# Activations streamed by even and then odd 64-byte lines in the 256-column projections

## The reference, cut to what matters

```python
def swiglu(h, w_gu, w_down):
    g, u = jnp.split(h @ w_gu, 2, axis=-1)
    return (jax.nn.silu(g) * u) @ w_down          # w_down: 2816 x 1024
# layers 0 and 1: h += .5*norm(swiglu(norm(h))); h += norm(mixer(norm(h))); h += .5*norm(swiglu(norm(h)))
# layer 2 (256 tokens):
merged = (jax.nn.sigmoid(gate_a) * (o_a @ w_br_dsa)       # 512 x 1024
          + jax.nn.sigmoid(gate_b) * (o_b @ w_br_moba))   # 512 x 1024
x = x + gt_m * (merged @ w_out)                           # 1024 x 1024
x = x + gt_f * ((jax.nn.silu(g_ff) * u_ff) @ w_down)      # 2816 x 1024
```

## Time and profile before

| | us |
|---|---|
| median of 3 runs | 1467.04 |
| the profiled execution | 1465.28 |
| its span, first to last instruction | 1463.4 |
| TensorE busy with MATMULs | 1441.8 (99%) |
| weight loads busy | 1403.4 (96%) |
| VectorE busy | 1055.0 (72%) |
| ScalarE busy | 700.6 (48%) |

### The profile page before, as it was taken

One profiled execution on the slowest core, in us unless ns is written; L12 is line 12 of the kernel. 1 busy time (PEld: TensorE's weight loads), 2 busy tenths in 40 slices (PEclk: granted clock), 3 DMA queues, 4 the chain that ended last, 5 costly groups with the idle time before them and its releaser, 6 DMA issues. The chain is left out here.

```text
span 1463.4 us, 28421 instructions
## 1 busy us (share of the span) xinstructions
PE 1441.8 (99%) x11567; PEld 1403.4 (96%) x11567; DVE 1055.0 (72%) x1431; ACT 700.6 (48%) x910; POOL 28.9 (2%) x58
## 2 busy tenths in 40 slices
PE   8999999999999999999999989999999999999999
PEld 8999999999999999999999889999987899999999
DVE  6766779777667786667778668767887777776652
ACT  6544353454443454443554656443446766644441
POOL 0000100000001000001000000001000000000000
PEclk9999999999999999999999999999999999999999
DMA  9555745437447644458343216557733436355550
GB/s 331 223 180 187 252 166 202 173 104 267 175 172 237 252 173 173 172 188 280 146 173 116 87 61 257 208 193 243 261 116 124 144 139 230 143 213 191 186 187 30
DMA packets 42538, 269.09 MB, mean 184 GB/s; under 512 B 4768, under 2 KB 5920, under 8 KB 13520
## 3 DMA queue, kind: packets, MB, share of 16 engines
q1 hardware_dynamic: 33984, 240.31, 45.3%
q0 software_dynamic: 7312, 26.44, 5.5%
q10 hardware_dynamic: 1152, 1.05, 0.2%
HBM read 266.73 MB, written 1.05 MB: 183 GB/s over the span
## 5 line engine op out<-in xcount | busy, mean ns | idle before, releaser
L418 PE MATMUL ps<-x_hi,w_hi 128*128 128x272 f32 (+2 forms) x2296 | 661.4, 288 | 5.0 <-DVE x_lo L1381 2.0
L419 PE MATMUL ps<-x_lo,w_hi 128*128 128x272 f32 (+2 forms) x2296 | 651.9, 284 | 0.0
L420 PE MATMUL ps<-x_hi,w_lo 128*128 128x272 f32 (+2 forms) x2296 | 651.9, 284 | 0.0
L2019 ACT ACTIVATE w_hi<-raw_weights 128x2048 fp32r<-128x2048 f32 x219 | 416.8, 1911 | 291.6 <-PE ps L420 288.9
L1175 DVE TENSOR_TENSOR w_lo<-raw_weights,w_hi 128x2048 fp32r<-128x2048 f32 x193 | 439.6, 2288 | 139.6 <-ACT w_hi L2019 139.1
L418 PEld LDWEIGHTS ps<-x_hi,w_hi 128*128 128x128 f32 x2296 | 433.3, 189 | 8.8 <-DVE x_lo L1381 2.8
L419 PEld LDWEIGHTS ps<-x_lo,w_hi 128*128 128x128 f32 x2296 | 433.2, 189 | 0.7
L420 PEld LDWEIGHTS ps<-x_hi,w_lo 128*128 128x128 f32 x2296 | 433.0, 189 | 0.0
L418 PE MATMUL ps<-a_hi,w_hi 128*128 128x272 f32 x592 | 169.6, 286 | 0.0
L419 PE MATMUL ps<-a_lo,w_hi 128*128 128x272 f32 x592 | 169.6, 286 | 0.0
L420 PE MATMUL ps<-a_hi,w_lo 128*128 128x272 f32 x592 | 169.6, 286 | 0.0
(11 more groups left out here) (258 smaller groups left out, 1537.6 us busy)
## 6 DMA issues: line engine op xcount, KB each, us to landing
raw_weights<-w_units SPq DMA_DIRECT2D x226, 1024.0 KB, 4.9
mod_w<-mod_units POOLq DMA_DIRECT2D x48, 512.0 KB, 5.7
raw_weights<-w_units SPq DMA_DIRECT2D x4, 256.0 KB, 5.1
raw_weights<-w_units SPq DMA_DIRECT2D x2, 512.0 KB, 8.2
out<-h ACTq DMA_DIRECT2D x8, 128.0 KB, 1.9
h<-x_in SPq DMA_DIRECT2D x2, 272.0 KB, 3.8
h<-x_in SPq DMA_DIRECT2D x1, 544.0 KB, 6.8
tab<-tables POOLq DMA_DIRECT2D x1, 512.0 KB, 6.7
```

The lines of the kernel that those rows point to most:

```text
L418: pe.matmul(dst, wh, hi, start=start, stop=False)
L419: pe.matmul(dst, wh, lo, start=False, stop=False)
L420: return pe.matmul(dst, wl, hi, start=False, stop=stop)
L2019: act.activation(w_hi[:, u % RING, :], raw[:, u % RING, :], ACT.Copy).then_inc(S["hi_ready"], 1)
```

## The change

In `k_outer`, where the stage has 256 columns, the three access patterns of a product (the output in PSUM, the hi and the lo activations) are rearranged alike. The 256 columns are seen as 8 pairs of 16-column runs, a run being 64 bytes: first come the first runs of all pairs, then the second runs. So each MATMUL takes lines 0, 2, 4, ... 14 of the activation row and then 1, 3, 5, ... 15, and writes each column to the place in PSUM where it stood before. The weights, the loads of weights, the number and order of the instructions and every semaphore stay as they are: TensorE's list has 7896 rows before and after. The 272-column stages, `attn_out`, and the gate, up and input projections are untouched.

```diff
@@ -527,6 +527,9 @@
+            def even_lines_first(columns):
+                return columns.rearrange("p (a b c) -> p b a c", b=2, c=16)
+
             def k_outer(st, xs, a_base, done=(), done_units=0, busy=None):
@@ -547,8 +550,10 @@
                             wait_bank(st, st.t0 + m)
                             if busy is not None and m in busy:
                                 busy[m]()
-                        ins = three_pass(ps[:, st.bank(st.t0 + m), 0:st.T], u % RING, (kk * 8 + m) * P,
-                                         xs[0][:, k, 0:st.T], xs[1][:, k, 0:st.T], k == 0, k == 2 * st.units - 1)
+                        dst, hi, lo = ps[:, st.bank(st.t0 + m), 0:st.T], xs[0][:, k, 0:st.T], xs[1][:, k, 0:st.T]
+                        if st.T == SEQ:
+                            dst, hi, lo = even_lines_first(dst), even_lines_first(hi), even_lines_first(lo)
+                        ins = three_pass(dst, u % RING, (kk * 8 + m) * P, hi, lo, k == 0, k == 2 * st.units - 1)
                         if k == 2 * st.units - 1:
                             ins.then_inc(S["tile_done"], 1)
```

## The result

The changed kernel takes 1475.43 us, the median of 3 runs (1474.61 to 1477.34), against 1467.04 before: a ratio of 1.0055, 95% interval 1.0031 to 1.0078. It is slower by 8.4 us; 4.6 us less had been forecast. The profiled execution took 1474.61 us with a span of 1472.7, against 1463.4. Three executions, two of the kernel before and one of the writes-only kernel, came out at a lower granted clock and far longer (1724.66 to 2024.59 us at 0.65 to 0.77 of it); all ratios and ranges here leave those out.

The account below looks back on a forecast made before the run. Bound by TensorE's pace in the changed stages: 708 MATMULs x 5.5 ns = 3.9 us and 732 x 1.0 = 0.7 us, in all -4.6 us, from 1467.04 to 1462.4 us. Range for 8 in 10: 1459.3 to 1475.5 us.

Parts of the forecast that it names:

- the prediction's own formula: In the five 256-column stages, the change costs 1440 x (V - 115.5), 115.5 ns being the mean distance before.
- V: Distance of MATMUL starts in the 256-column stages under the new order; taken as 112.3 ns, between 111.2 and 113.3.
- the slow way of lying: Timing of weight reads against activation reads in `down, 3` and `w_out`, claimed to give about 117.8 ns, not 113.3.
- Fewer meetings: In the 256-column stages, weight and activation reads collide less: V from 111.2 to 113.3, 1460.8 to 1463.9 us; chance 0.38.
- 106.7 ns: Figure for 256 columns to which the prediction added 2.5 ns to get 109.2.
- excesses of 1.7 and 3.3: Two values in ns, from rows 6 and 7, between which the prediction allowed 2.5 on top of 106.7 ns.
- 109.2: Distance in ns, 106.7 and 2.5, subtracted from the 113.3 of the quick stages.
- 4.1 to halve: In the quick stages, 113.3 - 109.2 ns taken as cost of colliding reads; half of it gives V = 111.2.
- Longer meetings: In the 256-column stages, the slower case of colliding reads; profile to show 118 ns; chance 0.20.
- By the pattern itself: In 256-column MATMULs, 15 jumps at one cycle add 6 ns, +8.6 us, 1475.7; chance 0.12 (costly jumps).
- No change: `down, 3` and `w_out` stay slow, the others quick, 1467.0 us; chance 0.30 with a mixture of stages within 2.9 us.
- one-cycle jump: In 256-column MATMULs, each jump of the pattern costs one 2.4 GHz cycle, 0.4 ns; 1475.7 us in all.

Follow-up runs that it names:

- writes-only kernel: Against the changed kernel, only the PSUM writes go even lines first and activations are read in natural order; 0.9993 of before (0.9977 to 1.0010).
- reads-only kernel: Against the changed kernel, only the activation reads go even lines first and PSUM is written in natural order; 1.0049 of before (1.0029 to 1.0068).
- moved weights: Against the kernel before, both weight tensors lie 64 bytes higher and what lies behind them 128, all orders natural; 1490.78 us, 1.0150 of before.
- 4-column window: Unit of `down, 3` whose products read the same 4 columns again and again, in place of the whole row; 111.9 ns, 111.7 in the single distances.
- the sweep: Against the changed kernel, each of the 11 units of `down, 3` and `down, 4` takes its own order; 117.7 to 123.3 ns by unit, no whole time given.

## Why the prediction was wrong

It had the place right, and all that was said of what stands around it. The stages run at TensorE's pace (MATMULs are under way in 99% of the span, before and after), so what a MATMUL loses is lost in the end: 1440 x (121.3 - 115.5) = 8.4 us by the prediction's own formula, and the traces have 8.2 in the five stages. That the medians differ by 8.4 as well is in part luck, since three runs a side don't fix them to a tenth; the reads-only kernel, at the same 121.3 ns, was 1.0049 of before, 7.2 us. That the reads of weights and activations bear on each other is shown by the moved weights. That this is the reason of the two speeds of one instruction, 113.3 and 117.8 ns, is not. The reading of the earlier trace rows for it was wrong: the load that starts together with the MATMUL at 994.75 is that MATMUL's own, after the wait, and in the quick stages too the load for the next MATMUL starts within 0.01 us of each MATMUL. The untouched stages kept their distances in the profile after.

The step that failed is the one that leads to V: "so half is V = 111.2; if only the slow way of lying disappears, V is 113.3". I took 112.3 between them, and 121.3 was measured. That the new order halves what two reads cost, the case "Fewer meetings" of the chances, was a guess of mine about which lines get into each other's way, and no row of the trace and no run bore it out. No run shows the other terms of that sum either: not the 106.7 ns for 256 columns, nor the excesses of 1.7 and 3.3 that are counted from such a figure, nor so the 109.2; the traces give the clock as a share of full speed, without a figure in GHz. What the traces show is 115 ns from start to start for 272 columns of bf16, 110 for transposes of 128 columns, and for 256 columns of fp32 111.7 at the least, in the 4-column window. The quick speed stands 1.6 ns above that least value, where the sum had 4.1 to halve. The runs show in place of the guess that the new order takes away the pace that natural order has. Four lines in turn, 256 bytes, go as quickly as the whole row (113.3 ns once settled). Orders that go back and forth on one or two lines in four, as the change does in each half, are at 118 to 123. This is a description and not yet a rule. Eight sweeps of 16 columns and sixteen of 8 pass the lines alike if only the number modulo four counts, and took 120.0 and 123.3; and the two-sweep order of 8 columns goes over the lines in turn, by half lines, and took 119.8.

Of the slower cases, "Longer meetings" (the two reads in each other's way for longer) gave the right sign and the right part of the machine; the profile was to show 118 for it, below the 121.3 that came. That a long stay on the same lines costs fits line 0 alone at 120.0 against the round of four at 113.3, but not the single 16 bytes at 111.9. "By the pattern itself" predicted the look of the result best, one distance in all stages over 119 ns, and with 1475.7 us its time; that was luck, for its reason is wrong, as the sweep shows: 3 jumps and 63 are both at 117.9, and no run shows a clock cycle, or 0.4 ns, for a jump. The sentence that would have read it off that distance misled. "No change" is out. The upper bound of 1475.5 was also said to go up to the one-cycle jump, which by the prediction's own sum is 1475.7.

What stays open is how the two reads come to bear on each other: why natural order has two distances, why a shift of the weights by two lines leaves natural alone and moves the even-first order, why the same shift or the same line had two values, and why even and odd halves cost 1.0 to 1.3 ns more together than their mean. The numbers above bound it and don't settle it.

## What to carry to other kernels

Where TensorE streams fp32-sized operands back to back with a weight load for each MATMUL, measure the distance of starts, not durations, and treat the order and the relative address of activations and weights as parameters: weights 64 bytes higher, with what lies behind them 128, moved this kernel by 1.5%. Keep the moving operand in plain ascending order over at least 256 bytes: here four lines in turn settled at 113.3 ns, as natural order does at its quick speed, and the nine other orders of the sweep took 117.9 to 123.3. A new order is cheap to try beforehand, unit by unit within one profile, as the sweep did with ten of them. Take natural order along in several units and read a value twice: natural order has two speeds here, 113.3 and 117.8 ns, and a unit's start still carries the one before it (113.8 over the last unit of the sweep, 113.3 in its second half).

## What the runs showed of the hardware

- One MATMUL of 256 columns with its weight load takes 111.7 to 123.3 ns (the 4-column window and sixteen sweeps of 8), by nothing but the order and place of what is read.
- Natural order is at 113.3 or 117.8 ns and stays there for hundreds of MATMULs; in `down, 3` it was slow after a stall and quick after six or twelve MATMULs in another order. What chooses the speed when a stage begins is open.
- A PSUM write in 64-byte runs out of order cost no time that could be measured (0.9977 to 1.0010 of before).
- The kernel before varies from 1462.3 to 1473.3 us between runs (the 21, 17 and 17 runs beside the experiments), more than in its first three. The lock is worth 3.2 us either way in the changed stages and 4.3 us in the up projection ahead of `down, 3`, which no order here touched.
